# Output projection of the chunk MLP over token slices of 512, 384 and 256 columns in place of three of 384

## The reference, cut to what matters

```python
def chunk_mlp_mixer(xn, w_in, g_v, w_s, b_s, w_out):
    uv = jax.nn.gelu(xn @ w_in)
    u, v = jnp.split(uv, 2, axis=-1)
    v = layernorm(v, g_v)
    ...
    sv = jnp.einsum('gts,bcsgd->bctgd', mix, vg) + b_s[:, :L].T[None, None, :, :, None]
    out = (u * sv.reshape(B, S, MLP_INNER)) @ w_out     # (1152 x 2048) @ (2048 x 1024)
    return out, v
# then: x = x + out; x = x + swiglu(rmsnorm(x), ...)
```

## Time and profile before

| | |
|---|---|
| Median of the three runs | 3070.45 us |
| Span of the profiled execution, first to last instruction | 3057.0 us |
| What lies around the span (median less span) | 13.4 us |
| PE busy | 2962.4 us, 97% of the span |
| DVE, POOL, ACT busy | 1590.3, 1066.8 and 404.2 us |
| Output projection, first to last matmul | 1973.4 to 2179.7 us |
| Matmuls of the projection | 1152, each 128x128 weights by 384 columns |

### The profile page before, as it was taken

The page is one execution under the profiler, slowest core; times in us unless marked ns, Lnnn a source line. Parts: engine busy times, 40 slices in busy tenths (PEclk is TensorE's granted clock), DMA queues, the critical chain, the costliest instruction groups (busy, mean ns, idle before and its releaser), DMA issues.

```text
span 3057.0 us, 42569 instructions
## 1 busy us (share of the span) xinstructions
PE 2962.4 (97%) x16838; PEld 2908.7 (95%) x16838; DVE 1590.3 (52%) x2335; ACT 404.2 (13%) x688; POOL 1066.8 (35%) x452
## 2 busy tenths in 40 slices
PE   7899999989999999999899999999999999999998
PEld 6899989889999999999899989999899999999998
DVE  6465563775555555555633365520455555555555
ACT  4112020320000000000311221300300000000004
POOL 4232232233333333333133223343433333333331
PEclk9999999989999999999899999999899999999999
DMA  2131121201111111111011111111111111111111
GB/s 91 42 69 39 49 44 48 43 28 42 42 41 41 41 41 41 41 43 41 25 42 40 33 58 43 34 41 42 42 35 42 41 41 42 46 43 41 41 41 62
DMA packets 198782, 133.27 MB, mean 44 GB/s; under 512 B 6714, under 2 KB 188602, under 8 KB 198714
## 3 DMA queue, kind: packets, MB, share of 16 engines
q1 hardware_dynamic: 198714, 132.27, 15.3%
HBM read 121.75 MB, written 10.50 MB: 43 GB/s over the span
## 4 chain that ended last, share of the span: by engine, by line
PE 92%; DVE 6%; issue 1%; ACT 0%; POOL 0%; DVEq 0%; POOLq 0%; ACTq 0%
PE ps L588 85%; DVE xn_lo L1296 2%; PE ps L1029 1%; DVE sq_f L1267 1%; PE ps L610 1%; PE ps L782 1%; PE ps L953 1%; PE ps L838 1%; PE ps L810 0%; PE ps L844 0%; PE ps L840 0%; PE ps L818 0%; DVE ssum_f L1268 0%; PE ps L733 0%; PE ps L621 0%
## 5 line engine op out<-in xcount | busy, mean ns | idle before, releaser
L588 PE MATMUL ps<-xn_hi,w_hi 128*128 128x384 f32 x3480 | 1194.4, 343 | 35.3 <-DVE xn_lo L1296 19.7
L544 POOL TENSOR_TENSOR w_hi<-w_raw,ones 128x1024 fp32r<-128x1024 f32 x213 | 532.2, 2498 | 1912.7 <-PE ps L588 1896.1
L588 PE MATMUL ps<-xn_hi,w_lo 128*128 128x384 f32 x3480 | 1182.3, 340 | 0.5 <-issue 0.5
L588 PE MATMUL ps<-xn_lo,w_hi 128*128 128x384 f32 x3480 | 1182.5, 340 | 0.0
L588 PEld LDWEIGHTS ps<-xn_hi,w_hi 128*128 128x128 f32 x3480 | 661.3, 190 | 43.3 <-DVE xn_lo L1296 17.5
L588 PEld LDWEIGHTS ps<-xn_lo,w_hi 128*128 128x128 f32 x3480 | 661.4, 190 | 0.5
L588 PEld LDWEIGHTS ps<-xn_hi,w_lo 128*128 128x128 f32 x3480 | 660.7, 190 | 0.0
L548 POOL TENSOR_TENSOR w_lo<-w_raw,w_hi 128x1024 fp32r<-128x1024 f32 x213 | 529.9, 2488 | 16.7
L1611 DVE TENSOR_TENSOR xT<-xT,ps 128x384 f32<-128x384 f32 x528 | 279.3, 550 | 172.3 <-PE ps L588 172.3
L588 PE MATMUL ps<-hg_hi,w_hi 128*128 128x384 f32 x1056 | 358.0, 339 | 0.0
L588 PE MATMUL ps<-hg_hi,w_lo 128*128 128x384 f32 x1056 | 356.0, 337 | 0.0
(11 more groups left out here) (265 smaller groups left out, 2361.5 us busy)
## 6 DMA issues: line engine op xcount, KB each, us to landing
w_raw<-in_f_w_gu_dram SPq DMA_DIRECT2D x88, 512.0 KB, 3.8
w_raw<-in_f_w_down_dram SPq DMA_DIRECT2D x44, 512.0 KB, 3.5
w_raw<-in_b_w_in_dram SPq DMA_DIRECT2D x32, 512.0 KB, 4.1
w_raw<-in_a_w_in_dram SPq DMA_DIRECT2D x24, 512.0 KB, 4.1
w_raw<-in_b_w_out_dram SPq DMA_DIRECT2D x16, 512.0 KB, 4.2
out_dram<-y_out SPq DMA_DIRECT2D x9, 512.0 KB
x_in<-in_x_prompt_dram SPq DMA_DIRECT2D x8, 512.0 KB, 5.5
c_nat<-in_state_C_dram SPq DMA_DIRECT2D x8, 512.0 KB, 5.9
```

Of the source, the lines that this page charges most:

```text
L544: nc.gpsimd.tensor_tensor(w_hi[s][:, :, :], w_raw[r][:, :, :], ones[:, :].unsqueeze(1).to_broadcast([P, KD, P]), ALU.mult)\
L588: ins = pe.matmul(out, w[slot][:, k, :], x(k), start=(first and n == 0), stop=(last_one and n == total - 1))
```

## The change

The three groups of the output projection are no longer the groups of 384. `BO_CUTS` cuts the nine tiles at 0, 4, 7 and 9, so the slices have 4, 3 and 2 tiles: 512, 384 and 256 columns. The number of matmuls stays 1152 and so does the sum of their columns. The low and high parts are still made in pieces of 384 tokens in the order `P_ORDER`. A slice now waits for the piece of the last group that it touches: slice 0 (tiles 0 to 3) reaches into group 1, slices 1 and 2 end in group 2. The adds to `xT` follow the slices.

```diff
@@ -87,6 +87,14 @@
 P_ORDER = [(g, f) for a in range(2) for g in range(NG) for f in range(KD * a, KD * (a + 1))]
+
+
+BO_CUTS = [0, 4, 7, NT]
+
+
+def bo_tiles(s):
+
+    return BO_CUTS[s], BO_CUTS[s + 1]
@@ -1042,17 +1050,20 @@
                 for u in range(4):
                     j, a = u // 2, u % 2
                     pe.wait_ge(split, W_BO.count(i, u, 1))
-                    for g in range(NG):
+                    for s in range(len(BO_CUTS) - 1):
+                        c0, c1 = bo_tiles(s)
+
                         def ready(k):
 
-                            pe.wait_ge(ps_lo, P_ORDER.index((g, KD * a + k)) + 1)
+                            last_group = (c1 - 1) // TPG
+                            pe.wait_ge(ps_lo, P_ORDER.index((last_group, KD * a + k)) + 1)
 
                         if a == 0:
 
-                            pe.wait_ge(bo_add, i * 6 + 3 * j + g + 1)
-                        ins = passes(bank(3 * j + g), W_BO.slots[u], range(KD),
-                                     lambda k: tok(p_hi[:, KD * a + k, :], g),
-                                     lambda k: p_lo[:, TPG * g:TPG * (g + 1), KD * a + k, :], a == 0, a == 1, g == 0,
+                            pe.wait_ge(bo_add, i * 6 + 3 * j + s + 1)
+                        ins = passes(bank(3 * j + s, (c1 - c0) * P), W_BO.slots[u], range(KD),
+                                     lambda k: p_hi[:, KD * a + k, c0 * P:c1 * P],
+                                     lambda k: p_lo[:, c0:c1, KD * a + k, :], a == 0, a == 1, s == 0,
                                      ready)
                         if a == 1:
                             ins.then_inc(bo_mm, 1)
@@ -1727,10 +1738,11 @@
             with dve.Fori(0, KD // 2) as i:
                 for n in range(6):
-                    j, g = n // 3, n % 3
+                    j, s = n // 3, n % 3
+                    c0, c1 = bo_tiles(s)
                     dve.wait_ge(bo_mm, i * 6 + n + 1)
-                    out = tok(xT[:, :, :], g)[:, bass.ds(i * 2 + j, 1), :].rearrange("p o t -> p (o t)")
-                    dve.tensor_tensor(out, out, bank(n), ALU.add).then_inc(bo_add, 1)
+                    out = xT[:, :, c0 * P:c1 * P][:, bass.ds(i * 2 + j, 1), :].rearrange("p o t -> p (o t)")
+                    dve.tensor_tensor(out, out, bank(n, (c1 - c0) * P), ALU.add).then_inc(bo_add, 1)
```

## The result

The changed kernel took 3075.19 us (median of 12 runs, 3068.58 to 3087.44), the kernel before 3068.6 us (12 runs, 3061.52 to 3074.24). The ratio is 1.0028, with a 95% interval of 1.0015 to 1.0042. The medians lie 6.6 us apart. The ratio is that of the means, and its interval stands for 4.6 to 12.9 us. So the change makes the kernel slower by about a quarter of a percent, and the forecast was 10.0 us. Another 12 runs on another chip gave 1.0028 again (1.0014 to 1.0041), with medians of 3069.17 us against 3061.24.

A forecast was written before the change was run, and what follows sets the result against it. PE bounds the kernel, busy 97% of the span. Unit 1's late split +7.5, cold clock +2.6 and last add -0.1 sum to +10.0 us, giving 3080.4 us; 8-in-10 range 3069 to 3085, forecast's own range 3077 to 3083.

The forecast's parts named there:

- The step that decided: POOL's split of unit 1 waits until DVE's low pieces are through, so unit 1 starts 7.5 us later.
- PE's first matmul: Projection's first matmul wants piece 9 in place of 1 and starts 3.75 us later; two later waits go.
- The cold clock: After idling, PE restarts at clock 0.50, losing 2.6 us in unit 0 and again in unit 1.
- The last add: Final add on the path has 256 columns in place of 384: -0.1 us.
- The columns: Projection matmuls of 512, 384 and 256 columns take time in proportion: 0, bounds -5 to +22 us.
- the bound on the floor: Limit on the least time of a 256-column projection matmul, from plain float32 rows: 0.121 us, +2 us.
- Rival A: POOL's split of unit 1 enters at the first handover near 1978, no loss: 3070.2 us; chance 0.29 with C.
- Rival B: A floor under the 256-column matmuls in all 16 units, up to +22 us; chance 0.09.
- C: PE's clock stays warm through 6.9 us idle before unit 0; matters only with A, then 3068; joint chance 0.29.

The follow-up runs named there:

- the waits alone: Kernel before with 384-wide groups kept, each group waiting for the low piece the changed slices would want; ratio 1.0007.
- the pause: Changed kernel, but DVE stops after 16 of its 48 low pieces until POOL has split unit 1; 3058.24 us, ratio 0.9978.
- the three late releases: Kernel before, with the matmul that lets POOL go on moved to block 4, 5 or 7 of each unit; single runs 3083.38, 3063.72 and 3088.95 us.

## Why the prediction was right

- **The step that decided held.** POOL was kept out of its w_hi for DVE's whole run: 19.4 us, where some 19 were forecast. The wait ahead of unit 1 is 8.04 us (8 forecast), and the shift of unit 1 is 7.3 us (7.5). All seven executions in which POOL came for unit 1 at piece 9 or later of an unbroken run show it: the changed kernel twice, the waits alone, the pause (until the pause) and the three late releases. In the other seven the next split comes between pieces 33 and 43 and is kept out to the last piece as well (w_hi of 5.0 to 9.4 us).
- **PE's first matmul** moved by 3.75 us (3.75), and the two waits of the earlier trace rows went.
- **The cold clock** cost 2.55 us in unit 1 (2.6), with 5.4 us at 0.50. In unit 0 it was 4.4 us at 0.50, which cost about 2.0 us (2.6), hidden by the wait for unit 1. The bounds of 3.4 and 8 us that the forecast's own range used for this stretch come from no row.
- **The last add** took 0.42 us in place of 0.56 (-0.1 forecast).
- **The columns.** 0 was the term. The mean durations of 512, 384 and 256 columns in the changed kernel are about 395, 339 and 280 ns, so 128 columns make 56 to 59 ns at either end, and there is no floor under the narrow ones. A unit takes 12.56 us with the new slices and 12.48 without, where matmuls run at their closer spacing (12.67 and 12.72 at the wider one). That is +1.3 or -0.8 us over 16 units. The forecast had misread on the way: line 789 issues nine matmuls and the trace has 18 records, so a plain float32 matmul is two records here, and the 0.121 us are those of one record. Each record has its own weight load, so the bound on the floor stood all the same.

These are the rows for it, of the changed kernel from 2018.5 to 2195 us (busy us, mean ns of one | idle):

```profile
L596 PE MATMUL ps<-p_hi,w_lo 128*128 128x512 f32 x112 | 44.3, 395 | 0.0
...
L596 PE MATMUL ps<-p_lo,w_hi 128*128 128x384 f32 x112 | 38.0, 339 | 0.0
...
L596 PE MATMUL ps<-p_lo,w_hi 128*128 128x256 f32 x110 | 30.8, 280 | 0.0
```

- **Rival A fell** (POOL in at the first handover), and with it the Trainium skill's rule as far as it speaks of the handover ("SBUF — State Buffer", section "SBUF: two separate sides"). That one side stands still while the other works is seen in every run here (a piece of 2.7 us, or a w_hi of 5 to 20). That the one kept out comes in when the other's instruction ends is not: 36 pieces went by in the changed kernel. **Rival B fell** with the rows above. **C** had nothing for it: the clock was at 0.50 in unit 0.
- **What was off.** The level. I put 13.4 us around the span, as the median less one span. A profiled execution's own time is 1.7 us above its span (3080.28 and 3078.6 after), so the profiled execution before took about 3058.7, a quick one. This doesn't touch the forecast of 3080.4 us, which is also the median plus 10.0. It was 5.2 us too high: some 1.9 us because the median of three runs lay above that of twelve, and the rest because the medians differ by 6.6 us and not by 10.0.
- **How well the 10.0 us are shown.** In the stage the traces account for 7.3 + 2.55 - 0.1 = 9.7 us of the terms forecast, and 1.2 more by the slices. The times say 6.6 us by the medians and 4.6 to 12.9 by the interval. That is the right sign and size, but the times alone wouldn't tell 10 us from 6.

## What to carry to other kernels

Before you make an engine wait longer for its first input, look at what its start releases. Here a wait of 3.75 us was paid back by saved stalls, but it moved POOL's release from the third piece of a VectorE run to the twelfth, and that cost about 10 us in the trace. Where VectorE does a long unbroken run of operations with two SBUF operands, GpSimd's work should be done before it, or the run should have a gap: one wait in the middle of it, a third weight slot, or another order of the pieces took the loss away.

## What the hardware showed that I had not expected

- **Who gets the shared port depends on how far DVE's run has come.** POOL got in beside pieces 3, 4 and 5 of an unbroken run, and was kept out at pieces 9, 10, 12 and 15, and for pieces 35 to 48 in the kernel before. Once out, it stayed out in all 14 executions until the run ended or paused, and then needed its usual 2.2 to 2.4 us. Where between pieces 6 and 9 the line lies, and why, stays open.
- **Warm matmuls have two spacings.** With the clock at 1.00 throughout, 50 us of 384-column float32r matmuls hold 290 of them or 285. A unit of 72 takes 12.48 or 12.72 us, that is 0.1733 or 0.1767 us for each. Matmuls of 512 columns are spaced 0.233 us in both cases. A kernel changes between the two within one execution, for tens to hundreds of microseconds, and not at the same places in two executions. This window is of the kernel before and then of the changed one, in a stage that the change doesn't touch:

```profile
1850.00:1900.00 50.00, 50.00 (x290) 50.00 (x289) 26.06 (x41) 6.98 (x13) 20.02 (x9) 1.00 0.15 42
```

```profile
1850.00:1900.00 50.00, 50.00 (x285) 50.00 (x284) 25.07 (x40) 6.98 (x13) 19.04 (x8) 1.00 0.15 42
```

  Over the program's 15,000 such matmuls, 3.3 ns each could make up to 50 us. Summed over each trace, what the warm matmuls of 384 columns take above 0.1733 us each comes to 20 us in the kernel before, 28 in the changed one, and 14 to 37 us over the 14 profiled executions. So some 8 of the 21.6 us between the two spans are of this kind. The runs of one kernel spread by 13 to 25 us in the sets of 11 or more runs, and two kernels that differ by 4 us can't be told apart by a dozen runs. The spacing need not be all of it: of the changed kernel's 12 runs the quickest (3068.58 us) has the highest mean granted clock, 0.983, and the slowest (3087.44 us) has 0.979. What sets the spacing wasn't tried.
